# Moving the last 4096 columns of a hand-placed memory plan by 96 columns

## The reference

```python
def reference(x, c, ctx, ...):
    x = first_block(x, c, ctx, ...)     # latent attention, gated scan, Fourier mix, then
    return second_block(x, mem_2, ...)  # window attention, RWKV-7 scan, memory attention, then

# the part of each block that the change touches, cut to its products
y = concatenate([attn, hg, fn]) @ w_out            # 1024 x 1024 x 1024
x_new = x + g1 * y
x_new = x_new + g2 * (silu(gate) * up) @ w_dn      # gate, up = h @ w_gu, hidden width 2816
# second block: proj = h @ w_in (heads and RWKV inputs), out projection, and
# a gated FFN whose up projection passes a causal convolution of width 3
```

## Time and profile before

| | |
|---|---|
| median of three runs | 3350.35 us (3342.61 to 3350.71) |
| profiled execution, its own time | 3350.35 us |
| its span in the profile | 3348.5 us |
| PE busy | 3169.7 us, 95% of the span |
| DVE, ACT, POOL busy | 1455.5, 1054.2, 371.0 us |
| mean granted TensorE clock | 0.982 of full speed |
| DMA | 182.33 MB, mean 54 GB/s |

### The profile page before, as it was taken

One profiled execution on the slowest core, in us unless ns is written; L12 is line 12 of the kernel. 1 busy time (PEld: TensorE's weight loads), 2 busy tenths in 40 slices (PEclk: granted clock), 3 DMA queues, 4 the chain that ended last, 5 costly groups with the idle time before them and its releaser, 6 DMA issues.

```text
span 3348.5 us, 42666 instructions
## 1 busy us (share of the span) xinstructions
PE 3169.7 (95%) x18680; PEld 2440.9 (73%) x18680; DVE 1455.5 (43%) x2104; ACT 1054.2 (31%) x1616; POOL 371.0 (11%) x390
## 2 busy tenths in 40 slices
PE   6999999999899999999998988998889999999999
PEld 2456666666667888888887766676777888888887
DVE  6256634576444211112336544266753443344333
ACT  4233322443323211112114655334433322222211
POOL 1012202343212100000001100011111100000000
PEclk9989999999999999999999999999999999999999
DMA  6011110000023111111212201000013111110212
GB/s 245 32 63 64 63 66 13 26 14 13 13 76 133 56 50 51 51 40 36 101 44 88 80 19 38 19 6 3 2 42 127 60 39 50 51 51 32 101 46 74
DMA packets 35209, 182.33 MB, mean 54 GB/s; under 512 B 4261, under 2 KB 4261, under 8 KB 21584
## 3 DMA queue, kind: packets, MB, share of 16 engines
q1 hardware_dynamic: 22176, 133.18, 11.3%
q0 software_dynamic: 12848, 46.43, 3.6%
HBM read 161.63 MB, written 17.96 MB: 54 GB/s over the span
## 4 chain that ended last, share of the span: by engine, by line
PE 85%; DVE 8%; ACT 4%; DMA 1%; issue 1%; POOL 1%; DVEq 0%; POOLq 0%; ACTq 0%; SPq 0%
PE ps L548 17%; PE ps L550 17%; PE ps L549 17%; PE ps L538 10%; PE ps L687 4%; PE ps L751 3%; PE ps L592 2%; PE ps L1228 2%; DMA ar<-in_xT 1%; PE ps L651 1%; PE ps L1089 1%; PE ps L834 1%; PE ps L609 1%; DVE ar L2089 1%; ACT ar L1449 1%
## 5 line engine op out<-in xcount | busy, mean ns | idle before, releaser
L548 PE MATMUL ps<-r,r 128*128 128x512 f32 x2632 | 1034.2, 393 | 10.7 <-DVE r L2085 5.4
L549 PE MATMUL ps<-r,r 128*128 128x512 f32 x2632 | 1025.9, 390 | 0.0
L550 PE MATMUL ps<-r,r 128*128 128x512 f32 x2632 | 1025.8, 390 | 0.0
L548 PEld LDWEIGHTS ps<-r,r 128*128 128x128 f32 x2632 | 495.1, 188 | 125.2 <-issue 16.2
L549 PEld LDWEIGHTS ps<-r,r 128*128 128x128 f32 x2632 | 495.1, 188 | 104.4 <-issue 3.0
L550 PEld LDWEIGHTS ps<-r,r 128*128 128x128 f32 x2632 | 494.9, 188 | 103.5
L2078 DVE TENSOR_TENSOR r<-ar,r 128x1024 fp32r<-128x1024 f32 (+1 forms) x170 | 204.6, 1204 | 325.0 <-ACT r L1411 324.9
L1411 ACT ACTIVATE r<-ar 128x1024 fp32r<-128x1024 f32 (+1 forms) x170 | 174.4, 1033 | 535.2 <-PE ps L550 495.4
L1449 ACT ACTIVATE ar<-ps 128x256 f32<-128x256 f32 (+3 forms) x330 | 146.9, 470 | 540.7 <-PE ps L538 119.2
L538 PE MATMUL ps<-ar 128*128 128x128 f32 (+4 forms) x1460 | 248.5, 343 | 6.4 <-ACT ar L1449 3.3
L538 PEld LDWEIGHTS ps<-ar 128*128 128x128 f32 (+1 forms) x1460 | 193.8, 188 | 57.5 <-issue 31.8
(11 more groups left out here) (295 smaller groups left out, 3495.5 us busy)
## 6 DMA issues: line engine op xcount, KB each, us to landing
ar<-in_w_mod SPq DMA_DIRECT2D x24, 1024.0 KB, 4.9
ar<-in_w_gu SPq DMA_DIRECT2D x22, 1024.0 KB, 4.8
ar<-in_w_up SPq DMA_DIRECT2D x22, 1024.0 KB, 4.8
ar<-in_w_in SPq DMA_DIRECT2D x19, 1024.0 KB, 4.8
ar<-in_w_dn SPq DMA_DIRECT2D x32, 512.0 KB, 3.4
x<-ar POOLq DMA_DIRECT2D x48, 256.0 KB, 2.4
ar<-x POOLq DMA_DIRECT2D x24, 512.0 KB, 7.9
ar<-in_xT POOLq DMA_DIRECT2D x16, 512.0 KB, 12.7
```

What stands on the lines that cost most here:

```text
L548: M.matmul(o, whk, hi[k][:, a:a + n], start=k == 0, stop=False)
L549: M.matmul(o, whk, lo_[k][:, a:a + n], start=False, stop=False)
L550: ins = M.matmul(o, wlk, hi[k][:, a:a + n], start=False, stop=k == nk - 1)
```

## The change

`TAIL` was `COLS - 4192`, column 48992. It left 96 columns at the end of `ar` that no tile from `TAIL` on used. The name is dropped and `COLS - 4096`, column 49088, stands in its place: the four tiles of homes 0 and 1 and, in the RWKV stage, `PP` and `toks` each start 96 columns (384 bytes) later, and the last of them ends with the array. The limits of three other regions move with it; no tile of these is placed elsewhere.

```diff
-TAIL = COLS - 4192
...
-    wh = rounded(TAIL, 2)
-    wl = rounded(TAIL + 2048, 2)
+    wh = rounded(COLS - 4096, 2)
+    wl = rounded(COLS - 2048, 2)
...
-    r5 = Region(FT + 8192, TAIL)
+    r5 = Region(FT + 8192, COLS - 4096)
...
-    r5 = Region(stage_at, TAIL)
+    r5 = Region(stage_at, COLS - 4096)
...
-    assert r9.at <= TAIL
+    assert r9.at <= COLS - 4096
     halves = [[r8.tile(512) for _ in range(6)] for _ in range(2)]
-    r8 = Region(TAIL)
+    r8 = Region(COLS - 4096)
```

## The result

The changed kernel is slower. Its four runs took 3383.55 to 3391.39 us, median 3388.20; four runs of the kernel before, the three named above among them, had a median of 3348.53 us. The ratio is 1.012 with a 95% interval of 1.0105 to 1.0135, so some 40 us. I had forecast 3350 us, 3341 to 3359, and given "slower" 0.06. The measured time is far outside the range.

What follows compares the result with a forecast made beforehand. Half the kernel was taken as a float32r matmul stream on TensorE that waits for nobody. To 3350.35 us the matmuls from homes 0 and 1, the splits and the RWKV stage each added 0: 3350 us, range 3341 to 3359.

Steps and rivals of the forecast that it cites:

- What bounds the kernel: Lines 548 to 550, 51% of the chain: a float32r matmul stream that waits for nobody, one matmul each 226.7 ns.
- the splits: Rounding on ACT and subtracting on DVE into homes 0 and 1: taken as 0, covered; 2.9 us if the cover were gone.
- the RWKV tiles: Copies into moved tiles and 576 matmuls of lines 1290, 1292, 1295: taken as 0, bounds 8.5 us either way.
- the first part: The 6936 matmuls with weights in homes 0 and 1: taken as 0, bounds 13.9 us either way.
- equality of two places: Blocks of 24 matmuls took 5.44 us with weights at 32 (out projection) and at 864 (down projection), 226.7 ns a matmul.
- the ring: Slots at the new place, 960 modulo 1024 columns: float32 loads 190 ns and matmuls 592 ns there, so no loss shown.
- the load's 38.7 ns to spare: At lines 548 to 550 a weight load takes 188 ns against the 226.7 ns interval, so it doesn't set it.
- 24 whole lines: The move of 384 bytes is 24 lines of 16 bytes in SBUF, so engine accesses meet their lines as before: 0.
- Rival (a): Slower at lines 548 to 550: weights at 960 read less well beside the moving operand; 3364 us by 2 ns, chance 0.06.
- upper price of 7 ns a matmul: Slower matmuls from homes 0 and 1 by the whole spread of loads, 186 to 193 ns: 48.6 us, 3399 us, held remote.
- Rival (b): Faster matmuls from homes 0 and 1: 864 has a loss, 960 none; 3336 us by 2 ns, at most 3257; chance 0.06.
- the 13.4 ns above one column a cycle: Matmul interval of 226.7 ns less 213.3 for 512 columns; if all the address's doing, 92.9 us to be had.

## Why the prediction was wrong

**What bounds the kernel** was right: half of it is the stream of lines 548 to 550, which waits for nobody, and its interval sets the time. That no instruction, wait or DMA moves was right too; so were the splits (1.06 and 1.23 us), the RWKV tiles (218 ns), and the statement that an address can act only through the duration of instructions.

**The step that failed** is the first part, the matmuls with weights in homes 0 and 1, taken as 0 with bounds of 13.9 us either way. It measured 39.9 us, 5.75 ns for each of 6936 matmuls. Three things went wrong in it.

First, I read equality of two places as indifference to place. The blocks of the earlier trace rows are equal, and I wrote that one place is in step with the activations and the other not. But weights at 32 and at 864 columns are 832 apart, and 832 is 13 times 64 columns: with respect to the activations both are in step modulo 256 bytes. The kernel before had no float32r pair out of step, so its trace held one case twice. The new place is 960 - 32 = 928 columns off, 14.5 times 64. I had compared places modulo 1024, and never asked modulo what the two compared ones were the same.

Second, I took the ring as the witness for the new place, in float32. The form makes the difference: float32 with the ring's tiles shows 429 ns whatever the distance, in the kernel as alone, and float32r doesn't.

Third, the load's 38.7 ns to spare were no protection. The load didn't grow past 226.7 ns; its mean stayed at 188 to 189. Nor do the 38.7 ns measure anything to spare, since loads with records of 192 ns can follow each other every 111.1 ns (rows of 128 columns). The Trainium skill says in "TensorE: Matmul & The Clock Gate", step-by-step section, that loading the next tile's weights doesn't steal SBUF read bandwidth from the running matmul. By that rule the sum would have stayed at 3350 us; the measured interval depends on where the one tile stands to the other, by 5.75 ns, and the measurement decides. The same holds for the 16-byte lines that the Trainium skill gives in "SBUF — State Buffer", specifications, by which I took 24 whole lines to change nothing: a distance of one whole line, 16 bytes, had 233.3 ns.

**Rival (a)** is what happened, in its place and by one of the ways named ("as soon as the two reads delay each other at all"). Its chance of 0.06 was too low, and its price of 13.9 us came from the difference of two load durations, while the interval grew without the load's duration changing. Its upper price of 7 ns a matmul, which I called remote, was near: 5.75. The honest bound of a combination that no row shows was that price, not 2 ns, and the range should have reached to 3399 us; as it stood it left out even the 13.9 us that I had set as this part's bound. That 7 ns lay near 5.75 is luck, since it was a spread of load durations too. **Rival (b)** is refuted for this address: no distance tried had less than 226.7 ns with 512 columns, so the 13.4 ns above one column a cycle are not the distance's.

No version beats the kernel before. The changed kernel's layout with the activations moved by 128 bytes equals it.

## What to carry to other kernels

In a stream of float32r matmuls with 384 or 512 moving columns, keep stationary and moving tiles a multiple of 256 bytes apart; here that is worth 5.75 ns in 232.6, 1.2% of the kernel, and costs a few padding columns. When a tile moves, compare each pair of operands read together, before and after, in the form in which it is read: an equality in the trace is evidence only if the two cases differ in what could matter. And a combination that no row shows deserves a bound from the stream's own interval, not from a neighbour's duration.

## What was not expected of the hardware

- The interval between two matmuls depends on the distance of the weight tile and the moving tile modulo 256 bytes: 226.7 to 227.2 ns at 0, 228.9 to 234.3 at most other distances, with no other engine at work. That the reads of the two tiles delay each other is my reading of it; why 256, and what collides, no run shows.
- The effect is that of float32r with 384 or 512 columns (2.6 and 5.7 ns at 128 bytes). With 128 columns it is 0.5 ns, with 256 the rows out of step were 1.2 and 2.0 ns shorter, and it is absent in float32 (429 ns) and in bf16 (215.8 ns).
- It is lopsided and has a memory: at 252 bytes the same pair of tiles ran at 226.7 or some 233 ns by what preceded it, and a single load out of step also lengthened the interval behind it, so that one such load in three cost some 70% of the whole loss (1.0085 against 1.012).
